# Gate tables of an expert layer: per-token scalar operations on packed bf16 tiles in place of broadcasts over four interleaved tokens

## The reference

```python
q = einsum('bsd,dq->bsq', h, w_q)                       # 8 heads, two halves of 128
scores = einsum('bshpc,hpnc->bshpn', q, sub_keys)       # 128 first keys, 128 second keys
top_s, top_i = top_k(scores, 16)
cand = top_s[first, :, None] + top_s[second, None, :]   # 256 pairs a head
best_s, best_pos = top_k(cand, 16)
expert = first_key * 128 + second_key                   # 16 of 16384 experts a head and token
gate = softmax(best_s)
act  = gelu(x . expert_u[expert])
y    = sum(gate * act * expert_v[expert])
```

## Time and profile before

| | |
|---|---|
| median of 3 runs | 1622.71 us (1620.39 to 1625.55) |
| the profiled execution's own time | 1624.48 us |
| its span, first to last instruction | 1623.2 us |
| PE busy | 1459.7 us, 90% |
| PE weight load busy | 1291.8 us, 80% |
| DVE busy | 950.2 us, 59% |
| ACT busy | 629.8 us, 39% |
| mean granted clock of PE | 0.933 of full speed |
| DMA | 317.39 MB, mean 196 GB/s |

### The profile page before, as it was taken

One profiled execution on the slowest core, in us unless ns is written; L12 is line 12 of the kernel. 1 busy time (PEld: TensorE's weight loads), 2 busy tenths in 40 slices (PEclk: granted clock), 3 DMA queues, 4 the chain that ended last, 5 costly groups with the idle time before them and its releaser, 6 DMA issues.

```text
span 1623.2 us, 19786 instructions
## 1 busy us (share of the span) xinstructions
PE 1459.7 (90%) x8518; PEld 1291.8 (80%) x8518; DVE 950.2 (59%) x1169; ACT 629.8 (39%) x540; POOL 32.3 (2%) x25
## 2 busy tenths in 40 slices
PE   6898659999979776769999889999998999999998
PEld 5777447888868665669999889999998777777776
DVE  6434436888443714456887558666644656565654
ACT  4334315443324344335434343333333444444441
POOL 0000010000000000000000000000000000000000
PEclk9898879999969966789999899999999999999999
DMA  8322035998414310324666357676777676777770
GB/s 322 136 104 102 2 147 193 380 374 329 163 52 148 111 65 0 130 80 155 238 223 237 132 171 236 206 216 210 213 254 288 255 289 260 284 261 282 270 275 26
DMA packets 83238, 317.39 MB, mean 196 GB/s; under 512 B 6096, under 2 KB 40144, under 8 KB 53200
## 3 DMA queue, kind: packets, MB, share of 16 engines
q1 hardware_dynamic: 83152, 316.14, 54.1%
HBM read 281.51 MB, written 34.60 MB: 195 GB/s over the span
## 4 chain that ended last, share of the span: by engine, by line
PE 74%; DVE 14%; ACT 8%; issue 2%; POOL 1%; DMA 0%; SPq 0%; ACTq 0%; DVEq 0%; POOLq 0%
PE psum L413 72%; DVE slab_lo L1228 6%; ACT slab_hi L878 4%; PE psum L416 2%; DVE arena L1786 1%; POOL statistics L407 1%; DVE arena L1487 1%; DVE x_lo L1790 1%; DVE residual L1292 0%; DVE arena L1246 0%; ACT arena L893 0%; DVE weighted_lo L1790 0%; ACT arena L882 0%; DVE arena L1263 0%; ACT L902 0%
## 5 line engine op out<-in xcount | busy, mean ns | idle before, releaser
L1228 DVE TENSOR_TENSOR slab_lo<-slab_raw,slab_hi 128x2048 fp32r<-128x2048 f32 x207 | 471.7, 2289 | 314.4 <-ACT slab_hi L878 296.6
L878 ACT ACTIVATE slab_hi<-slab_raw 128x2048 fp32r<-128x2048 f32 x207 | 393.7, 1909 | 307.9 <-PE psum L413 307.9
L413 PE MATMUL psum<-x_hi,slab_hi 128*128 128x256 f32 x1216 | 352.6, 290 | 23.2 <-DVE slab_lo L1228 13.3
L413 PE MATMUL psum<-x_lo,slab_hi 128*128 128x256 f32 x1216 | 349.5, 287 | 0.0
L413 PE MATMUL psum<-x_hi,slab_lo 128*128 128x256 f32 x1216 | 349.2, 287 | 0.0
L413 PE MATMUL psum<-slab_hi,x_hi 128*128 128x512 f32 x784 | 315.6, 403 | 20.7 <-DVE slab_lo L1228 6.7
L413 PE MATMUL psum<-slab_lo,x_hi 128*128 128x512 f32 x784 | 310.0, 395 | 0.0
L413 PE MATMUL psum<-slab_hi,x_lo 128*128 128x512 f32 x784 | 309.6, 395 | 0.0
L413 PEld LDWEIGHTS psum<-x_hi,slab_hi 128*128 128x128 f32 x1216 | 238.7, 196 | 24.7 <-issue 20.3
L413 PEld LDWEIGHTS psum<-x_lo,slab_hi 128*128 128x128 f32 x1216 | 238.6, 196 | 0.0
L413 PEld LDWEIGHTS psum<-x_hi,slab_lo 128*128 128x128 f32 x1216 | 238.3, 196 | 0.0
(11 more groups left out here) (231 smaller groups left out, 1181.1 us busy)
## 6 DMA issues: line engine op xcount, KB each, us to landing
slab_raw<-in_ex_u SPq DMA_DIRECT2D x64, 1024.0 KB, 5.8
slab_raw<-in_ex_v SPq DMA_DIRECT2D x64, 1024.0 KB, 5.1
arena<-in_w_ada SPq DMA_DIRECT2D x24, 1024.0 KB, 6.4
slab_raw<-in_w_in SPq DMA_DIRECT2D x22, 1024.0 KB, 4.8
slab_raw<-in_w_gu SPq DMA_DIRECT2D x22, 1024.0 KB, 6.8
hidden_store<-arena SPq DMA_DIRECT2D x32, 512.0 KB, 6.8
gates_store<-arena SPq DMA_DIRECT2D x8, 2048.0 KB, 9.3
arena<-hidden_store SPq DMA_DIRECT2D x32, 512.0 KB, 5.7
```

Of the source, the lines that this page charges most:

```text
L413: return PE.matmul(out, lhsT, rhs, start=start, stop=stop)
L878: ACTE.activation(slab_hi[:, slot, :], raw[:, slot, :], ACT.Copy).then_inc(hi_made[slot], 1)
L1228: DVE.tensor_tensor(slab_lo[:, slot, :], raw[:, slot, :], slab_hi[:, slot, :].bitcast(f32), ALU.subtract).then_inc(lo_made[slot], 1)
```

## The change

Key numbers are kept once (`keys`, 128 values) and no longer four times. `hit_b` and `gated` hold each token's 128 values side by side, and `hit_a` is gone. DVE now issues, for each of the 8 tokens of a step, one tensor-scalar instruction for `hit_b` (keys compared with a scalar per partition) and three for the parts of `gated` (compared with one scalar per partition, multiplied by a second), which are 32 instructions of 128 elements a step in place of five. PE's 24 matmuls a step are the same but read packed operands. `hit_b` lies in the space of `wf` instead of `zs`.

Besides this, steps change place. The exponential goes from ACT's step 24 to 20; the copies of ACT from steps 26, 30 and 33 to 23, 28 and 32; the copy of the second keys goes ahead of that of the third gate part; PE's transposes go from steps 25, 29 and 33 to 23, 27 and 31. `weigh(0)` moves from behind `lo` of the third `expert_v` slab to behind that of the first (DVE's s = 60), `weighted_hi(0)` from behind ACT's loop to its step 61, and `weighted_low(0)` stays behind `lo` of the third `expert_v` slab, inside the loop. The pace `gates_due` and all else are as before.

```diff
-        key4 = sb("key_numbers_by_4", [P, NKEYS, 4], bf16)
+        keys = sb("key_numbers", [P, NKEYS], bf16)
...
-        hit_b = zs[:].bitcast(bf16).rearrange("p (n g b t) -> p n g b t", n=2, g=2, t=4)
-        hit_a = wf[:].bitcast(bf16)[:, 0:1024].rearrange("p (g a t) -> p g a t", g=2, t=4)
-        gated = [[carve(8192 + 1536 * n + 768 * g, 768).bitcast(bf16).rearrange("p (q a t) -> p q a t", q=3, t=4)
-                  for g in range(2)] for n in range(2)]
+        hit_b = [wf[:, 512 * n:512 * n + 512].bitcast(bf16).rearrange("p (t b) -> p t b", t=8) for n in range(2)]
+        gated = [carve(8192 + 1536 * n, 1536).bitcast(bf16).rearrange("p (t q a) -> p t q a", t=8, q=3)
+                 for n in range(2)]
...
-                            ins = mm(ps[:, 4 + 2 * n + g, j * P:j * P + P], hit_b[:, n, g, :, j], gated[n][g][:, q, :, j],
-                                     q == 0, q == 2)
+                            ins = mm(ps[:, 4 + 2 * n + g, j * P:j * P + P], hit_b[n][:, 4 * g + j, :],
+                                     gated[n][:, 4 * g + j, q, :], q == 0, q == 2)
...
-                if s == 25:
+                if s == 23:
                     PE.wait_ge(*after("scores_copied", 4))
                     selection(4, sg_, "gate_softmax_made")
-                if s == 29:
+                if s == 27:
                     selection(5, sa, "first_keys_made")
-                if s == 33:
+                if s == 31:
                     selection(6, sbb, "second_keys_made")
...
                 hi(S_EU + s + 4)
-                if s == 24:
+                if s == 20:
                     ACTE.wait_ge(*after("gate_differences_made", 1))
                     ACTE.activation(sg_, sg_, ACT.Exp).then_inc(sem("gate_exp_made"), 1)
-                if s == 26:
+                if s == 23:
                     ACTE.wait_ge(*after("gate_softmax_made_transposed", 1))
...
-                if s == 30:
+                if s == 28:
                     ACTE.wait_ge(*after("first_keys_made_transposed", 1))
...
-                if s == 33:
+                if s == 32:
+                    ACTE.wait_ge(*after("second_keys_made_transposed", 1))
+                    ACTE.activation(sel_b[:], ps[:, 6, 0:S], ACT.Copy).then_inc(sem("choice_copied"), 1)
                     ACTE.wait_ge(*after("gate_rest_made", 2))
                     ACTE.activation(gate_parts[:, 2, :], zs[:, 2 * S:3 * S], ACT.Copy).then_inc(sem("gate_part_made"), 1)
-                    ACTE.wait_ge(*after("second_keys_made_transposed", 1))
-                    ACTE.activation(sel_b[:], ps[:, 6, 0:S], ACT.Copy).then_inc(sem("selected_keys_copied"), 1)
...
-            weighted_hi(0)
+                if s == 2 * EX_N - 3:
+                    weighted_hi(0)
...
             def gate_step(i):
                 n, t0 = i % 2, 8 * i
-                of_b, of_a, of_gated = [P, NKEYS, 4], [P, 2, NKEYS, 4], [P, 3, NKEYS, 4]
                 if i >= 2:
                     DVE.wait_ge(*after("hits_used", 2 * (i - 2) + 2))
-                for g in range(2):
-                    DVE.tensor_tensor(hit_b[:, n, g], key4[:],
-                                      sel_b[:, t0 + 4 * g:t0 + 4 * g + 4].unsqueeze(1).to_broadcast(of_b), ALU.is_equal)
-                if i:
-                    DVE.wait_ge(*after("gated_hits_made", 2 * i))
-                V(DVE.tensor_tensor(
-                    hit_a, key4[:].unsqueeze(1).to_broadcast(of_a),
-                    sel_a[:, t0:t0 + 8].rearrange("p (g t) -> p g t", g=2).unsqueeze(2).to_broadcast(of_a),
-                    ALU.is_equal))
-                V.after()
-                for g in range(2):
-                    DVE.tensor_tensor(
-                        gated[n][g], hit_a[:, g].unsqueeze(1).to_broadcast(of_gated),
-                        gate_parts[:, :, t0 + 4 * g:t0 + 4 * g + 4].unsqueeze(2).to_broadcast(of_gated),
-                        ALU.mult).then_inc(sem("gated_hits_made"), 1)
+                for j in range(8):
+                    t = slice(t0 + j, t0 + j + 1)
+                    DVE.tensor_scalar(hit_b[n][:, j, :], keys[:], sel_b[:, t], None, ALU.is_equal)
+                    for q in range(3):
+                        ins = DVE.tensor_scalar(gated[n][:, j, q, :], keys[:], sel_a[:, t], gate_parts[:, q, t],
+                                                ALU.is_equal, ALU.mult)
+                    if j % 4 == 3:
+                        ins.then_inc(sem("gated_hits_made"), 1)
...
+            DVE.wait_ge(*after("choice_copied", 2))
             DVE.wait_ge(*after("gate_part_made", 3))
-            DVE.wait_ge(*after("selected_keys_copied", 2))
             for n in slab:
                 lo(n)
                 s = n - S_EU - 4
                 for i in range(gates_due(s + 1), gates_due(s + 2)):
                     gate_step(i)
+                if s == 2 * EX_N - 4:
+                    weigh(0)
                 if s == 2 * EX_N - 2:
+                    weighted_low(0)
                     break
...
-            weigh(0)
-            weighted_low(0)
             lo(next(slab))
```

More of the change, by code:

```diff
@@ L1168, in copy_gates, with weighted_hi @@
                     sem("gates_copied"), 1)
+            def weighted_hi(c):
+                ACTE.wait_ge(*after("weighted_made", c + 1))
+                if c in (1, 2):
+                    slab_done(ACTE, S_EV - 1)
+                if c >= 3:
+                    slab_done(ACTE, S_EV + 2 * (c - 3) + 1)
+                ACTE.activation(w_hi[c % 3], hidden_in[c % 3], ACT.Copy).then_inc(sem("weighted_hi"), 1)
             for s in range(2 * EX_N):
@@ L1186, in scalar_program @@
                     ACTE.activation(gate_parts[:, 0, :], zs[:, 0:S], ACT.Copy).then_inc(sem("gate_part_made"), 1)
-                if s == 30:
+                if s == 28:
                     ACTE.wait_ge(*after("first_keys_made_transposed", 1))
-                    ACTE.activation(sel_a[:], ps[:, 5, 0:S], ACT.Copy).then_inc(sem("selected_keys_copied"), 1)
+                    ACTE.activation(sel_a[:], ps[:, 5, 0:S], ACT.Copy).then_inc(sem("choice_copied"), 1)
                     ACTE.wait_ge(*after("gate_rest_made", 1))
                     ACTE.activation(gate_parts[:, 1, :], zs[:, S:2 * S], ACT.Copy).then_inc(sem("gate_part_made"), 1)
-                if s == 33:
+                if s == 32:
+                    ACTE.wait_ge(*after("second_keys_made_transposed", 1))
+                    ACTE.activation(sel_b[:], ps[:, 6, 0:S], ACT.Copy).then_inc(sem("choice_copied"), 1)
                     ACTE.wait_ge(*after("gate_rest_made", 2))
                     ACTE.activation(gate_parts[:, 2, :], zs[:, 2 * S:3 * S], ACT.Copy).then_inc(sem("gate_part_made"), 1)
-                    ACTE.wait_ge(*after("second_keys_made_transposed", 1))
-                    ACTE.activation(sel_b[:], ps[:, 6, 0:S], ACT.Copy).then_inc(sem("selected_keys_copied"), 1)
                 for i in range(gates_due(s - 1), gates_due(s)):
                     copy_gates(i)
[L1201 to L1207, removed]
-            weighted_hi(0)
+                if s == 2 * EX_N - 3:
+                    weighted_hi(0)
             for c in range(EX_N):
@@ L1604, in vector_program @@
                 ins.then_inc(sem("residual_added"), 1)
-            DVE.tensor_copy(key4[:], iota[:].unsqueeze(2).to_broadcast([P, NKEYS, 4]))
+            DVE.tensor_copy(keys[:], iota[:])
             x_scale(PEER, 0)
@@ L1751, in gate_step @@
                 n, t0 = i % 2, 8 * i
-                of_b, of_a, of_gated = [P, NKEYS, 4], [P, 2, NKEYS, 4], [P, 3, NKEYS, 4]
                 if i >= 2:
                     DVE.wait_ge(*after("hits_used", 2 * (i - 2) + 2))
-                for g in range(2):
-                    DVE.tensor_tensor(hit_b[:, n, g], key4[:],
-                                      sel_b[:, t0 + 4 * g:t0 + 4 * g + 4].unsqueeze(1).to_broadcast(of_b), ALU.is_equal)
-                if i:
-                    DVE.wait_ge(*after("gated_hits_made", 2 * i))
-                V(DVE.tensor_tensor(
-                    hit_a, key4[:].unsqueeze(1).to_broadcast(of_a),
-                    sel_a[:, t0:t0 + 8].rearrange("p (g t) -> p g t", g=2).unsqueeze(2).to_broadcast(of_a),
-                    ALU.is_equal))
-                V.after()
-                for g in range(2):
-                    DVE.tensor_tensor(
-                        gated[n][g], hit_a[:, g].unsqueeze(1).to_broadcast(of_gated),
-                        gate_parts[:, :, t0 + 4 * g:t0 + 4 * g + 4].unsqueeze(2).to_broadcast(of_gated),
-                        ALU.mult).then_inc(sem("gated_hits_made"), 1)
-            DVE.wait_ge(*after("gate_part_made", 3))
-            DVE.wait_ge(*after("selected_keys_copied", 2))
[L1773 to L1779, removed]
+                for j in range(8):
[6 more added lines that the diff above has]
+                        ins.then_inc(sem("gated_hits_made"), 1)
             def weigh(c):
@@ L1791, in weighted_low @@
                     sem("weighted_lo"), 1)
```

(14 more changed lines are left out.)

## The result

The changed kernel takes 1646.5 us in the median (1642.2 to 1647.4, 4 runs) against 1621.6 us (1620.4 to 1625.6, 4 runs) of the kernel before: ratio 1.0138, 95% interval 1.0121 to 1.0154. It is slower by 1.4%. The forecast, 1600 us and faster, is missed, and in direction as well: the time is that of rival B (1645), inside the stated range of 1582 to 1655 but on the other side of the kernel before. The profiled execution took 1642.2 us, the shortest of the four; its span is 1640.9 us.

What follows compares the result with a forecast made beforehand. PE was taken to bound the kernel, with three holes; the moves save 25.7 us from 1623.2 (1597.5), and DVE's dearer gate steps, just filling PE's old pace, give 1598 plus 2 for slip: 1600 us, range 1582 to 1655.

Steps and rivals of the forecast that it cites:

- rival B: DVE gate steps: the second scalar is read serially, adding about 60 ns; 1645 us, chance 0.29.
- second scalar: DVE gate steps, 24 of 32 instructions: a second per-partition scalar costs nothing more; bounds nothing or another 60 ns.
- the third move: Earlier first weighting at the start of expert_v: removes a 5.2 us hole and 1.9 us of half clock, 7.1 us.
- One-scalar price, 163 ns: DVE gate steps: 33 ns for 128 elements plus 130 ns fixed, taken for every tensor-scalar.
- Exponential at step 20: ACT's earlier exponential ends DVE's 22.5 us wait and PE's first hole, at 906.6; saves 10.0 us.
- Copies and transposes: Earlier steps remove PE's second hole, at 969.3; saves 8.6 us, with lo(34) done only 0.7 us before needed.
- the sum: DVE starts three low parts at 955.9, ends the gate stage's work at 1175.9; span 1598 us, plus 2 for slip.
- First weighting: Start of expert_v: weighting steps moved earlier let PE go on without its 5.2 us hole; saves 7.1 us.
- All moves: The three holes before the gate stage and at expert_v's start go; 25.7 us saved together, 1597.5 us if nothing else changed.
- Gate matmuls on PE: Gate stage: packed operands take 60 to 118 ns a matmul, worth 0 to 44.5 us if DVE keeps up.
- DVE bounds the stage: Gate stage: DVE needs 5.2 us a step against 3.2, 20.0 us per two slabs and three steps, using all spare time.
- Rivals C and E: C: DVE instructions at 119 ns or less, 1553 to 1597 us, 0.11; E: holes stay, 1607 to 1625 us, 0.05.

Runs made afterwards that it cites:

- float32 keys: The changed kernel with key numbers read from a float32 tile in place of the bf16 one: 1683.5 us, ratio 1.0372 to the kernel before.
- packed reads: Moved steps with DVE's old gate steps, but PE reads both gate-matmul operands as if packed, so tables hold wrong values: 1552.8 us, ratio 0.9569.

## Why the prediction was wrong, and where

**The step that failed** is the term "second scalar": "I take nothing more, as the nearest rows have the same form with one". It measures 60 ns, the upper of its two bounds: three two-scalar instructions take 0.67 us from start to start, and 0.49 us with a constant in place of the second scalar. So the price of 24 of the 32 instructions is 223 ns and not 163. 768 of them make 46 us. The forecast named it as the choice on which the sign hangs, and the run with a constant in its place shows that it does: 1602 us against 1646. The row that should have weighed more stood beside it: the first scalar adds 60 ns to the distance between starts, so its read was already not overlapped with anything. That speaks for reads that come one after another; I gave it 0.29 against 0.47. The range held the result only because its upper end was drawn from this rival.

That the run with a constant comes within 2 us of the forecast is in part luck. The forecast added 2 us for two engines at the same pace, but by its packed matmuls PE needed 15.6 us for two slabs and three steps, not 20.0, and so was never close to DVE; the third move, for its part, gave less than its 7.1 us (below). The two errors nearly cancel.

**Point by point:**

- *One-scalar price, 163 ns* (130 fixed, 33 for 128 elements): 163 measured. The float32 keys show the 33 for the elements by themselves; the 130 is what is left.
- *Exponential at step 20*: right. DVE's wait of 22.5 us is gone, and so are PE's hole and the half clock behind it. The timeline of DVE in the changed kernel has the reduction behind its low part without a wait:

```profile
881.71 2.29 DVE L1228 TENSOR_TENSOR slab_lo<-slab_raw,slab_hi 128x2048 fp32r<-128x2048 f32 x1 [0.29 <-ACT slab_hi L877]
883.92 0.41 DVE L1703 TENSOR_REDUCE statistics<-arena 128x16 f32<-128x256 f32 x1
```

- *Copies and transposes*: right, thin margin included. The second keys and the last gate part are copied directly behind ACT's `hi` of step 32, and DVE waits for them but PE does not wait for DVE:

```profile
949.51 1.92 ACT L877 ACTIVATE slab_hi<-slab_raw 128x2048 fp32r<-128x2048 f32 x1 [3.14 <-PE psum L412]
951.34 0.36 ACT L1201 ACTIVATE selected_second_keys<-psum 128x256 bf16<-128x256 f32 x1
951.60 0.41 ACT L1203 ACTIVATE selected_gates_in_parts<-hidden 128x256 bf16<-128x256 f32 x1
```

  The copy ends at 952.0, 2.5 us after the start of that `hi`, as forecast. DVE starts its three low parts at 952.09, 3.8 us before the time in the sum, because this execution reached the layer that much sooner.
- *First weighting*: right in kind, too large in size. PE goes from `expert_u` to `expert_v` at 1265.2 without a hole, but then waits 1.8 us for the second c (11.0 us busy of 12.8 in the last stretch above). The chain in the changed kernel names the low part of a slab and, behind it, `weighted_low(1)` (L1771; the tile is called `x_lo`):

```profile
1274.55 2.29 DVE slab_lo L1228
1276.85 1.15 DVE x_lo L1771
1278.03 23.84 PE psum L412 x100
```

  From the end of `expert_u` to the end of the span it is 1640.9 - 1265.2 = 375.7 us; before it was 1623.2 - 1241.6 = 381.6, and the sum had 374.5. So 5.9 us were saved and not 7.1. In the run with the moves alone it was 1601.9 - 1224.2 = 377.7, only 3.9 saved. 1.6 us of the difference are the granted clock, which fell after PE's wait in that execution and not in the other. The same 100 matmuls, first in the changed kernel and then with the moves alone:

```profile
1278.03:1301.87 23.84, 23.83 (x100) 18.70 (x100) 14.82 (x9) 8.02 (x6) 0.00 (x0) 1.00 0.70 271
1237.00:1262.48 25.48, 25.46 (x100) 19.84 (x100) 14.82 (x9) 8.06 (x6) 0.00 (x0) 0.93 0.67 253
```

- *All moves*: 25.7 us forecast, 23 measured when run alone. Most of what is missing is this third term.
- *Gate matmuls on PE*: the bounds were 60 and 118 ns. 56 measured, just under the lower one. The Trainium skill ("SBUF — State Buffer", Door 1) lets bf16 be strided for free within a 16-byte line, that is up to eight elements. By it the time would have stayed at 118. The measurements disagree for the moving operand: its step of four elements, 8 bytes, takes twice the time of a packed one, and the step of two next to nothing (58 ns). They agree for the weights, whose step of four costs no time.
- *DVE bounds the stage*: right, though with other numbers. The arithmetic of rival B, 962.6 + 32 x 6.66 + 46.3, put the last table at 1222; less the 3.8 us above it is 1218, and the last of the 768 instructions starts at 1217.9. The fall of the clock cost nothing, as DVE had no wait in the stage.
- *Rivals C and E*: the one-scalar price was 163 ns and not under 119, and the first two holes were gone, so both fall.
- *Slips in the sums*, none of which matters here: with the second scalar serial the terms add up to 33 + 130 + 60 = 223 ns, not 226 or 224; from 1600 to the kernel before are 23 us and not 25, so break-even is a mean of 185 ns, or a second scalar of 30; and at a price of 150 ns the sum gives 1585, not 1582.
- *The table's estimate for one instruction, 94 ns* (the Trainium skill, "VectorE: DVE Perf Modes", The TRN2 errata: 58 cycles + 128/4): too low for this form by 69 ns with one scalar and by 129 with two. The advice of the same section against many small tiles was right here: of the 163 and 223 ns only 33 are the elements.

**What the change gave and took**, from runs: moves -23 us, gate steps +45. Inside the gate steps PE's matmuls alone would give -47 (packed reads against the moves alone), but only while DVE stays under 15.6 us for two slabs and three steps. It needs 14 with the old instructions and 24.4 with the new ones (2 x 2.2 + 3 x 6.66).

## What to carry to other kernels

Price a small instruction by the distance between starts and not by its length, and count each operand read per partition as its own term; if one such read shows as unhidden time in a row, assume that a second costs the same again. When a layout is to suit both its writer and its reader, look for the smallest interleaving that keeps the writer's rate, and find out which of the reader's operands minds: here pairs gave DVE its doubled bf16 rate and PE its full one. And time a bundle's parts separately: the moves here were worth 23 us alone and hid half of what the new gate steps cost.

## What the runs showed of the hardware that was not expected

- A second scalar per partition in a VectorE tensor-scalar instruction costs another 60 ns between starts: 163 ns with one scalar (and with one scalar and a constant), 223 ns with two, at 128 bf16 elements; 196 and 256 ns with float32 elements.
- A 128 x 128 x 128 bf16 matmul takes 56 ns between starts with a packed moving operand, 58 ns in the kernel that reads both operands with a step of two elements, and 118 ns with a moving operand read with a step of four. The weights' step of four alone leaves it at 56 ns.
- Interleaving by two keeps the bf16 tensor-tensor rate on VectorE: 1024 elements take 0.69 us with an innermost run of two, the same as with four.
